# Differential attention with six product banks, turned in PSUM, its divisor in the norm behind it, and Pool's residual in two passes

## What is computed

```python
q = rope((hx @ wq).reshape(B, L, H, 2, d))      # H = 8 heads, two halves of d = 64
k = rope((hx @ wk).reshape(B, L, H, 2, d))
v = (hx @ wv).reshape(B, L, H, 2 * d)
kc, vc = hc @ wk, hc @ wv                       # 256 context tokens, not turned
lam = exp(sum(lq1 * lk1)) - exp(sum(lq2 * lk2)) + lam_init
p = softmax(q @ [k, kc].T * d ** -0.5)          # for each of the two halves
o = (p[0] - lam * p[1]) @ [v, vc]
o = o * rsqrt(mean(o ** 2) + 1e-5) * subln_g * (1 - lam_init)
out = o @ wo
x = layer_norm(alpha * x + g1 * out)
```

## Time and profile before

| quantity | us |
|---|---|
| median of 3 runs | 2900.06 |
| lowest and highest run | 2891.44, 2900.72 |
| profiled execution | 2902.76 |
| its span in the trace | 2900.9 |
| TensorE busy in it | 2693.1 (93%) |
| VectorE, ScalarE, Pool busy | 1292.1, 695.4, 1348.6 |
| the four rounds of the differential attention | 2041.8 to 2436.0 |

### The profile page before, as it was taken

How to read it: one execution, slowest core, us unless ns; L and a number is a source line. 1 busy time by engine, 2 the same in 40 slices (tenths; PEclk the granted TensorE clock), 3 DMA queues, 4 the chain that set the end, 5 groups by cost and what they waited for, 6 DMA issues and landing times.

```text
span 2900.9 us, 39349 instructions
## 1 busy us (share of the span) xinstructions
PE 2693.1 (93%) x14668; PEld 2160.6 (74%) x14668; DVE 1292.1 (45%) x1868; ACT 695.4 (24%) x1295; POOL 1348.6 (46%) x862
## 2 busy tenths in 40 slices
PE   7989999989999989899899999999688888999997
PEld 6667777767777768566778888887566766778886
DVE  6932222261222272445354444445755645345545
ACT  2221000041000033665120111101455644111112
POOL 6356555446555542234364333433522321586662
PEclk9999999999999999899999999999799998999999
DMA  5124444434444421000111111111000100222221
GB/s 186 44 81 155 145 144 144 145 115 149 145 145 145 145 90 63 1 1 1 59 51 59 58 63 60 58 58 58 29 30 29 43 29 15 73 94 94 94 94 58
DMA packets 67369, 235.57 MB, mean 81 GB/s; under 512 B 8144, under 2 KB 9552, under 8 KB 67152
## 3 DMA queue, kind: packets, MB, share of 16 engines
q1 hardware_dynamic: 65792, 233.64, 24.6%
q10 hardware_dynamic: 1488, 0.69, 0.1%
HBM read 232.21 MB, written 2.10 MB: 81 GB/s over the span
## 4 chain that ended last, share of the span: by engine, by line
PE 81%; DVE 8%; issue 4%; ACT 3%; POOL 2%; DMA 1%; DVEq 0%; SPq 0%; ACTq 0%; POOLq 0%
PE ps L577 63%; PE ps L1043 2%; PE ps L1071 2%; PE ps L970 2%; PE ps L768 2%; PE ps L732 2%; PE ps L956 1%; PE ps L1093 1%; DVE X L1945 1%; POOL X L554 1%; PE ps L696 1%; DMA raw<-in_stream 1%; DVE q L1992 1%; DVE X L1578 1%; DVE Alo L1567 1%
## 5 line engine op out<-in xcount | busy, mean ns | idle before, releaser
L447 POOL TENSOR_SCALAR whi<-raw 128x1024 fp32r<-128x1024 f32 x332 | 368.2, 1109 | 1231.5 <-DMA raw<-in_stream 1231.4
L449 POOL TENSOR_TENSOR wlo<-raw,whi 128x1024 fp32r<-128x1024 f32 x332 | 816.6, 2460 | 27.7
L577 PE MATMUL ps<-Ahi,whi 128*128 128x512 f32 (+1 forms) x2128 | 732.5, 375 | 67.4 <-DVE tmp L1836 25.5
L577 PE MATMUL ps<-Alo,whi 128*128 128x512 f32 (+1 forms) x2128 | 725.5, 372 | 0.0
L577 PE MATMUL ps<-Ahi,wlo 128*128 128x512 f32 (+1 forms) x2128 | 722.4, 371 | 0.0
L577 PEld LDWEIGHTS ps<-Ahi,whi 128*128 128x128 f32 x2128 | 377.3, 191 | 163.1 <-issue 28.0
L577 PEld LDWEIGHTS ps<-Ahi,wlo 128*128 128x128 f32 x2128 | 377.9, 191 | 71.3
L577 PEld LDWEIGHTS ps<-Alo,whi 128*128 128x128 f32 x2128 | 378.4, 191 | 66.8
L577 PE MATMUL ps<-hhi,whi 128*128 128x512 f32 x1120 | 376.8, 374 | 19.6 <-DVE X L1945 18.5
L577 PE MATMUL ps<-hhi,wlo 128*128 128x512 f32 x1120 | 372.5, 370 | 0.0
L577 PE MATMUL ps<-hlo,whi 128*128 128x512 f32 x1120 | 372.2, 369 | 0.0
(11 more groups left out here) (264 smaller groups left out, 2915.4 us busy)
## 6 DMA issues: line engine op xcount, KB each, us to landing
raw<-in_stream SPq DMA_DIRECT2D x428, 512.0 KB, 3.7
X<-in_xT SPq DMA_DIRECT2D x2, 1024.0 KB, 6.5
arena<-in_dft SPq DMA_DIRECT2D x1, 2048.0 KB, 16.5
out_xT<-X SPq DMA_DIRECT2D x2, 1024.0 KB, 4.3
X<-in_ctxT SPq DMA_DIRECT2D x1, 1024.0 KB, 19.0
w<-in_stream SPq DMA_DIRECT2D x2, 512.0 KB, 4.4
vec<-in_vec SPq DMA_DIRECT2D x1, 364.5 KB, 7.6
arena<-in_fmap SPq DMA_DIRECT2D x1, 256.0 KB, 12.1
```

The lines of the kernel that those rows point to most:

```text
L447: pool.tensor_scalar(whi[:, s, part], raw[:, s, part], 1.0, 1.0, ALU.mult, ALU.mult).then_inc(sem("w_hi"), 1)
L449: pool.tensor_tensor(wlo[:, s, part], raw[:, s, part], whi[:, s, part], ALU.subtract).then_inc(sem("w_split"), 1)
L577: mm = pe.matmul(dst[c], w[:, b % RING, off:off + P], rhs(k, part, c0, n), start=(k == 0 and w is whi and part == 0), stop=(k == kn - 1 an ...
```

## The change

The six products get a bank each, `QK_BANKS`, and no longer wait for `qkB_free`. Their first waits are now that the scores' banks (`sB_free`) and bank 4 (`aT`) of the round before have been read; the wait for `oB` moves to the front of the values, with `l2_kept`. The rotation works in place in PSUM, and `query_hi`, `key_hi`, `query_lo` and `key_lo` read PSUM, so that `rot` and two copies of context keys a round go. ScalarE's `key_hi(0)` moves ahead of `key_swap(1)`, VectorE's `key_lo(0)` ahead of the fourth turn. The inverse roots of "l2" move to banks 6 and 7.

The first half is no longer divided by its sum. VectorE's factor for the second half becomes first sum over second sum times lambda, and the inverse first sum goes to `over0` (a reciprocal more in each unit), which the norm behind the loop uses in three small products on 128x32. Lambda is clamped once (one more operation at the front). The semaphore counts that ScalarE and VectorE add once move ahead of the MLP. Pool's `norm_residual` makes all products first and then all scalings, in "l1", "l2" and "l3".

```diff
+QK_BANKS = (2, 3, 4, 5, 0, 1)
-RSTD = {"n1": 7, "n2": 5, "n4": 5, "n5": 3, "l1": 4, "l2": 4, "l3": 4, "l4": 3}
+RSTD = {"n1": 7, "n2": 5, "n4": 5, "n5": 3, "l1": 4, "l2": 6, "l3": 4, "l4": 3}
...
+        def q_turned(m):
+            return ps[:, QK_BANKS[m], :]
+        def k_turned(m):
+            assert QK_BANKS[3 + 2 * m] == QK_BANKS[2 + 2 * m] + 1
+            return psf[:, QK_BANKS[2 + 2 * m] * 512:QK_BANKS[2 + 2 * m] * 512 + TT]
...
             # Pool, norm_residual
-                for i in range(KT + 1):
-                    if i < KT:
-                        pool.tensor_tensor(X[:, i, 0:width], X[:, i, 0:width], rstd[:, 0:width], ALU.mult).then_inc(sem(f"{name}_y"), 1)
-                    if i >= 1:
-                        pool.wait_ge(*when(f"{name}_y", i))
+                for i in range(KT):
+                    pool.tensor_tensor(X[:, i, 0:width], X[:, i, 0:width], rstd[:, 0:width], ALU.mult).then_inc(sem(f"{name}_y"), 1)
+                for i in range(KT):
+                    pool.wait_ge(*when(f"{name}_y", i + 1))
...
             # TensorE
-                pe.wait_ge(*when("oB", 2 * st + 1))
+                pe.wait_ge(*when("sB_free", 16 * st + 2))
+                pe.wait_ge(*when("aT", 8 * st + 1))
...
-                            pe.wait_ge(*when(f"qkB_free{job % 2}", 3 * st + job // 2 + 1))
...
-                                mm = product([ps[:, 6 + job % 2, 0:n]], [(c0, n)], B_QKV + which, k * 256 + m * P, a_rhs, k, KT)
+                                mm = product([ps[:, QK_BANKS[job], 0:n]], [(c0, n)], B_QKV + which, k * 256 + m * P, a_rhs, k, KT)
...
-                for m in range(2):
-                    pe.wait_ge(*when(f"qkB_free{m}", 3 * st + 4))
+                pe.wait_ge(*when("l2_kept", 1))
+                pe.wait_ge(*when("oB", 2 * st + 1))
...
             # ScalarE: query_hi and key_hi read q_turned(m) and k_turned(m)
-                    copy(rot[:, m, T:TT], ps[:, 7, 0:C]).then_inc(sem("qkB_free1"), 1)
...
-                        act.wait_ge(*when("denB", 16 * st + 2 * u - 1))
-                        p0 = probB[(u - 1) % 3]
-                        copy(p0, p0, sm[:, (u - 1) % 4, 4:5]).then_inc(sem("p0B"), 1)
...
             # VectorE
-                    rotate(rot[:, r % 2, 0:T], ps[:, bank, :], scale, swapB[:, r % 2, :], (f"qkB_free{bank - 6}", 3 * st + free),
+                    rotate(ps[:, bank, :], ps[:, bank, :], scale, swapB[:, r % 2, :], ("cosB", 4 * st + r + 1),
                            ("sinB", 4 * st + r + 1), "qkB")
...
-                    dve.reciprocal(c[:, 4:6], c[:, 2:4]).then_inc(sem("denB"), 1)
+                    dve.reciprocal(c[:, 5:6], c[:, 3:4]).then_inc(sem("denB"), 1)
                     dve.wait_ge(*when("denB", 2 * unit + 1))
-                    dve.tensor_tensor(c[:, 6:7], c[:, 5:6], lamt[:, 5:6], ALU.mult).then_inc(sem("denB"), 1)
+                    dve.scalar_tensor_tensor(out=c[:, 6:7], in0=c[:, 5:6], scalar=c[:, 2:3], in1=lamt[:, 5:6], op0=ALU.mult,
+                                             op1=ALU.mult).then_inc(sem("denB"), 1)
...
-                    dve.wait_ge(*when("p0B", unit + 1))
...
+                    dve.reciprocal(over0[:, bass.ds(unit, 1)], sm[:, u % 4, 2:3])
...
-            dve.tensor_scalar(hnorm[:, 0, :], ps[:, 4, 0:8 * QT], SUB_OVER, None, ALU.is_lt).then_inc(sem("oB_flag"), 1)
+            dve.tensor_tensor(hnorm[:, 1, :], ps[:, 4, 0:8 * QT], over0[:, :], ALU.mult).then_inc(sem("oB_own"), 1)
+            dve.wait_ge(*when("oB_own", 1))
+            dve.tensor_tensor(hnorm[:, 1, :], hnorm[:, 1, :], over0[:, :], ALU.mult).then_inc(sem("oB_own"), 1)
+            dve.wait_ge(*when("oB_own", 2))
+            dve.tensor_scalar(hnorm[:, 0, :], hnorm[:, 1, :], SUB_OVER, None, ALU.is_lt).then_inc(sem("oB_flag"), 1)
             dve.wait_ge(*when("oB_std", 1))
+            dve.tensor_tensor(hnorm[:, 0, :], hnorm[:, 0, :], over0[:, :], ALU.mult).then_inc(sem("oB_own"), 1)
             dve.reciprocal(hnorm[:, 1, :], hnorm[:, 1, :]).then_inc(sem("oB_r"), 1)
```

More of the change, by code:

```diff
@@ L61 @@
 SUB_SCALE = 2.0 ** -40
-SUB_CLAMP = 2.0 ** 30
+SUB_CLAMP = 2.0 ** 40
+LAM_CLAMP = 2.0 ** 100
 SUB_OVER = 2.0 ** 48
@@ L250, in build @@
         hnorm = sb("hnorm", [P, 2, 8 * QT])
+        over0 = sb("over0", [P, 8 * QT])
         maskb = sb("maskb", [P, 3, P], BF16)
@@ L1457, in key_hi @@
                     act.wait_ge(*when("qkB", 4 * st + m + 5))
-                    act.wait_ge(*when("qkB_free1", 3 * st + m + 3))
-                    if m == 1:
-                        act.wait_ge(*when("l2_y", KT))
-                    for t in range(2):
-                        mm = copy(kB[m][t][DH * t:DH * t + DH], rot[DH * t:DH * t + DH, m, :])
-                    mm.then_inc(sem("qkB_hi"), 1)
-                def key_swap(m):
-                    act.wait_ge(*when("qkB_done", 4 * st + 2 + 2 * m))
-                    swapped(ps[:, 6, :], 1.0, 2 + m)
                     if m:
@@ L1471, in key_swap @@
                         act.wait_ge(*when("qkB_done", 4 * st + 3))
-                    copy(rot[:, m, T:TT], ps[:, 7, 0:C]).then_inc(sem("qkB_free1"), 1)
+                    if m == 1:
+                        act.wait_ge(*when("l2_y", KT))
+                    for t in range(2):
+                        mm = copy(kB[m][t][DH * t:DH * t + DH], k_turned(m)[DH * t:DH * t + DH])
+                    mm.then_inc(sem("qkB_hi"), 1)
+                def key_swap(m):
+                    act.wait_ge(*when("qkB_done", 4 * st + 2 + 2 * m))
+                    swapped(ps[:, QK_BANKS[2 + 2 * m], :], 1.0, 2 + m)
                 act.wait_ge(*when("qkB_done", 4 * st + 1))
-                swapped(ps[:, 6, :], SCALE, 0)
+                swapped(ps[:, QK_BANKS[0], :], SCALE, 0)
                 act.wait_ge(*block_used(b))
-                swapped(ps[:, 7, :], SCALE, 1)
+                swapped(ps[:, QK_BANKS[1], :], SCALE, 1)
                 query_hi(0)
@@ L1966, in mlp, with turned @@
                     add_down(ML_IT - 1, B0 + ML_BLOCKS - 1, m)
-            mlp(0, "ml0", X_CTX)
-            dve.sem_inc(sem("qkB_free0"), 1)
-            dve.sem_inc(sem("qkB_free1"), 1)
             dve.sem_inc(sem("qkB"), 2)
             dve.sem_inc(sem("oB"), 1)
+            mlp(0, "ml0", X_CTX)
             layernorm("l2", X_CTX, 2)
             with dve.Fori(0, 4) as st:
-                def turned(r, bank, scale, free):
+                def turned(r, bank, scale):
                     dve.wait_ge(*when("swB", 4 * st + r + 1))
-                    if r >= 2:
-                        dve.wait_ge(*when("qkB_lo", 4 * st + r - 1))
-                    rotate(rot[:, r % 2, 0:T], ps[:, bank, :], scale, swapB[:, r % 2, :], (f"qkB_free{bank - 6}", 3 * st + free),
+                    rotate(ps[:, bank, :], ps[:, bank, :], scale, swapB[:, r % 2, :], ("cosB", 4 * st + r + 1),
                            ("sinB", 4 * st + r + 1), "qkB")
@@ L1989, in query_lo @@
                         rows = slice(DH * t, DH * t + DH)
-                        q_two = rot[rows, m, 0:T].rearrange("p (a n) -> p a n", a=2)
+                        q_two = q_turned(m)[rows].rearrange("p (a n) -> p a n", a=2)
                         for half in range(2):
```

30 lines of the change are left out of this document (15 added, 15 removed).

## The result

The changed kernel took 2847.76 us (median of 4 runs, 2841.01 to 2855.36) against 2897.45 (4 runs) for the kernel before: ratio 0.9829, 95% interval 0.9811 to 0.9846. That is 1.7% faster. In a later session five more runs gave 2849.40 and a ratio of 0.9839 (0.9813 to 0.9866).

The account below looks back on a forecast made before the run. TensorE, busy for 93% of the span, was taken to bound the kernel, so only its waits could give time back. Terms -29.3 - 12.7 + 1.2 + 0.7 = -40.1 us took 2900.06 to 2860.0, stated as 2861, range 2849 to 2877.

Parts of the forecast that it names:

- the start of a round: Rounds 2 to 4: TensorE's 1.20 us wait before a round's first product goes, 3.6 us over three rounds.
- Part 1: Rounds 2 to 4: six banks and turning in PSUM end TensorE's waits, first halves take 33.65 us; 29.3 us gained.
- rival (a): First halves: the chain of VectorE and ScalarE ends after the values, 1.5 us a round, total 2866; chance 0.12.
- Rival (b): First halves: PSUM sources don't escape Pool, so VectorE's low halves stay slow, 3.6 us a round, total 2875; chance 0.06.
- rival (e): First halves: banks don't free TensorE, something else (the weights) holds key 1's latents product; total 2887, chance 0.03.
- Rival (d): Slower than before: ScalarE's and VectorE's operations on banks TensorE fills cost 1.3 us more each; total 2909, chance 0.02.
- 42.12, 42.07 and 42.49 less that is 25.7 us: First halves of rounds 2 to 4 in the profile before, less 33.65 us each: 25.7 us gained.
- Part 3: The divisor: two of VectorE's added reciprocals a round lie in front of a maximum the scores need, +1.2 us.
- rival (c): Clock-slowed second halves, not the change's doing: all three slow adds 4 (2865), none takes 6 (2855); chance outside forecast 0.12.
- Part 2: Round 1's first half: Pool makes its eight products before the scalings, done at 2083.5, scores 12.7 us sooner.
- Part 4: Norm behind the loop and front: small products with `over0` cost +0.7 us; lambda's clamp and moved counts 0.
- the counts moved ahead are a few hundredths: 0: Front of the kernel: semaphore counts moved ahead of the MLP cost a few hundredths, taken as 0.

Follow-up runs that it names:

- e1: The kernel before, unedited, traced a second time: 2897.96 us.
- e5: The kernel before with only the change's 128-byte tile `over0` allocated, unused, in front of the mask tile: 2891.74 us.
- e6: The kernel before with only the one-off counts of ScalarE and VectorE moved ahead of the MLP: 2902.51 us.
- e12: The kernel before with an unused tile of 64 bytes a partition in front of the mask tile: 2889.25 us.
- e8: The changed kernel, unedited, run again: 2852.97 us.
- e10: The changed kernel, unedited, in a later session of 5 runs: 2849.40 us, ratio 0.9839 to the kernel before.
- e7: The changed kernel with the divisor as before (ScalarE's copies, both divisors in one reciprocal, no `over0` in the norm): 2841.61 us.
- e3: The changed kernel with six banks kept but the turned tiles written to SBUF (`rot`) as before, with the waits this needs: 2888.53 us.
- e4: The changed kernel with Pool's residual as before, product and scaling in turn, tile by tile: 2856.14 us.
- e9: The changed kernel with Pool's residual of l2 in front of the split of the block that frees next: 2840.28 us (5 runs), ratio 0.9809 to before.
- e11: The changed kernel with the tile `over0` allocated behind the arena, so the arena lies at its old place: 2854.28 us.

## Why the prediction was right in kind and 13 us too high

The steps that failed are sizes and one missing term, and the sum of them left the range: the first halves of before, taken from one execution (3.2 us too short); the start of a round, read as idle time alone (5.3 us and not 3.6); the reciprocals (0 and not 1.2); and the place of the arena, which stood in no term and is worth 4 us.

To lessen chance I compare means: before over five executions of its stage (the profile, e1, e5, e6, e12) with the changed kernel over three (the profile, e8, e10).

| stretch | before | after | gained | predicted |
|---|---|---|---|---|
| first half, round 1 | 58.3 | 45.1 | 13.2 | 12.7 |
| first halves, rounds 2 to 4 | 130.1 | 101.1 | 28.9 | 25.7 |
| four second halves | 203.0 | 196.0 | 7.1 | 3.6 less 1.2 |
| MLP ahead of the stage | | | 4.0 | 0 |
| behind the stage | 465.5 | 466.6 | -1.1 | -0.7 |

**Part 1, the first halves: right.** J0 to J5 and two value tiles were forecast at 33.65 us and take 33.70 to 33.73 in nine of nine. The chain of VectorE and ScalarE stays under the values, so rival (a) is out, if narrowly: its last low half ends 33.57 us after J0 in round 2. (The prediction's steps for that chain add up to 33.0, not the 33.1 written there; its second low half takes 0.96 and not 0.82.) Rival (b) is out by the 2.79 us beside Pool's split, and rival (e), since nothing holds J4. Rival (d) is out: a step of the turn that writes PSUM costs 0.70 us where one that writes SBUF costs 0.69. By that the 62 cycles of "VectorE: DVE Perf Modes" (The TRN2 errata) in the Trainium skill don't show in this kernel; as an estimate from that table they would be 0.065 us. The rule of the Trainium skill's page "SBUF — State Buffer" (Who interferes with whom), that VectorE with at most one SBUF input doesn't contend with Pool, the traces bear out: 2.79 us with one, 8.02 with two, in the same place.

**What failed in part 1 is the minuend.** The step "42.12, 42.07 and 42.49 less that is 25.7 us" took the first halves of one execution. In five executions they average 43.3 and never fall below 42.07, because the last low key can meet Pool's next split (e1) and because J4 takes 7.1 to 8.6 us behind its wait. The profile that I had was the shortest of the five. That is 3.2 us. The changed kernel has neither, and its halves repeat to 0.03 us.

**The start of a round was mis-sized.** "The 1.20 us in front of it goes" read the idle time in the earlier trace rows. What goes is more: TensorE can issue a product before the one ahead of it has ended. In e10 the twelve products with the values start at 2212.10 and take 5.41 us, to 2217.51, but J0 starts at 2216.95:

```profile
2212.10 5.41 PE L1055 MATMUL ps<-arena 128*128 128x512 f32 x12 [1.02 <-ACT arena L1141]
2216.95 0.79 PE L589 MATMUL ps<-Ahi,whi 128*128 128x512 f32 x1
```

From the first of the twelve to J0 it is 4.85 us; in before it was 6.61 (2145.75 to 2152.36). So 1.76 us a round go, 5.3 in three rounds and not 3.6. (J0 then takes 0.32 us longer, 5.87 to J1's start instead of 5.55; that stands in the first half, where the value tiles take 0.25 less than the forecast.) At full clock the second halves bear the 1.76 out: 48.1 to 48.4 us in rounds 2 and 3 of before, 46.4 to 46.7 after.

**Part 3 was sized at +1.2 and costs nothing** that e7 shows. The two reciprocals that I had put in front of a maximum don't delay it: the maxima of round 2's last units follow each other by 3.75 and 4.15 us in e10 and by 3.78 and 4.16 in e7, where one reciprocal a unit is left. Of the 7.1 us in the second halves 5.3 are the start of a round and 0 the reciprocals; the remaining 1.8 are the clock. Nearly all of it is round 4, which takes 49.8 to 54.3 us in the five executions of before (52.7 in e3) and 49.7 to 49.9 in all eight with tiles turned in PSUM. So the step on rival (c), that which rounds are slow is not for the change to say, holds for rounds 1 to 3 (e1, e8, e10); whether round 4's is chance or a gain of the change isn't shown. Its price was too small: "none takes 6", while the second halves of the same code spread over 10 us before (199.1 to 209.3 in the table's kernels with before's stage) and 7.7 after (191.7 to 199.5), and the profile before happened to be the slowest of its five.

**Part 2: right**, 13.2 for 12.7. Pool's eight products take 15.28 us (15.2 forecast) from 2062.65, and TensorE waits 8.39 ("8 to 9"). The product ends at 2077.9 rather than 2083.5, 5.15 us of it because the whole stage starts earlier. e4 splits the gain: 5.7 for the two passes alone, and e9 shows what was left on the same path.

**Part 4: right in kind.** VectorE needs 0.58 us more in front of the norm's last product (TensorE waits 1.80 for it, 1.22 before), of which 0.3 reach the output projection. Some 0.8 us more lie further behind the stage, in a stretch that the change doesn't touch but for Pool's order; e4 has the old order and the 0.8 as well, so it isn't that. It stays open.

**The step that was missing: "the counts moved ahead are a few hundredths: 0"** priced the front of the change, and e6 bears that out, but the tile was priced nowhere. It moves the arena by 128 bytes, and that is worth 4 us (e5, e11). It was not in any rival.

Together: 0.5 + 3.2 + 4.7 + 4.0 less 0.4 are 12.0 us more than the sum had. The runs of the two kernels differ by 49.7 us, 9.6 more than the 40.1 forecast; the stage of the changed kernel starts on average only 1.4 us earlier (2039.4 against 2040.8 in before, e1 and e6), so that 2.6 of the 4.0 don't reach the time: its executions were late ahead of the MLP (1453.7 to 1458.5 at the wait in front of it, against 1450.8 to 1452.9), by chance as far as is known. 12.0 less 2.6 is 9.4, which is what the runs show within 0.2. The forecast missed by 13.2: these 9.6, another 2.6 because the median of before fell from 2900.06 to 2897.45 with a fourth run, and 1.0 between the sum's 2860.0 and the 2861 that I gave.

## What to carry to other kernels

When VectorE is slow beside Pool, look at where its inputs lie: a result that is read again beside Pool's work is best left in PSUM, and giving TensorE more banks was worth 2 us of 10 a round here while VectorE was still held up (e3). A chain that meets another engine's work by chance has a time that varies; before subtracting from it, take it from several executions, since one profile can be the lucky or the unlucky one. When an edit moves tiles in memory, compare a stretch that it doesn't touch, and run the old kernel with the allocation alone.
